# One more buffer in each ring of gathered expert rows, its room taken from the scratch of the dynamic DMAs

## What is computed

```python
def one_block(xb):                                  # xb: a block of 128 tokens
    ...
    eidx = jnp.take_along_axis(cidx, pos, axis=-1)  # 8 heads x 16 experts of 16384, per token
    gate = jax.nn.softmax(best.astype(jnp.float32), axis=-1)
    u = expert_u[eidx]
    act = jax.nn.gelu(jnp.einsum('td,thkd->thk', xb, u).astype(jnp.float32), approximate=False)
    vv = expert_v[eidx]
    return jnp.einsum('thk,thkd->td', (gate * act).astype(xb.dtype), vv)
```

## Time and profile before

| | |
|---|---|
| median of 3 runs | 2238.71 us (2237.37 to 2243.49) |
| the profiled execution: its time | 2239.32 us |
| its span, first to last instruction | 2237.5 us |
| TensorE busy | 2163.7 us, 97% |
| VectorE busy | 1173.6 us, 52% |
| HBM traffic over the span | 411 GB/s |

### The profile page before, as it was taken

One profiled execution on the slowest core, in us unless ns is written; L12 is line 12 of the kernel. 1 busy time (PEld: TensorE's weight loads), 2 busy tenths in 40 slices (PEclk: granted clock), 3 DMA queues, 4 the chain that ended last, 5 costly groups with the idle time before them and its releaser, 6 DMA issues.

```text
span 2237.5 us, 35119 instructions
## 1 busy us (share of the span) xinstructions
PE 2163.7 (97%) x14132; PEld 1989.9 (89%) x14132; DVE 1173.6 (52%) x2085; ACT 300.4 (13%) x951; POOL 370.8 (17%) x414
## 2 busy tenths in 40 slices
PE   7999998799899999999999999999999999999997
PEld 5677776586689979999999999999999999999997
DVE  3200002844466548778786457878544444444445
ACT  2000002712220011111111012322100000000002
POOL 0000100023201012222222112222111111111210
PEclk9999999999999999999999999999999999999998
DMA  7999995299969888999999999999999999999996
GB/s 286 404 400 419 403 419 190 95 370 410 384 239 400 311 312 350 404 412 421 421 419 418 420 421 409 411 398 420 421 421 422 422 422 422 422 422 422 418 422 257
DMA packets 126062, 853.68 MB, mean 382 GB/s; under 512 B 14512, under 2 KB 24880, under 8 KB 38928
## 3 DMA queue, kind: packets, MB, share of 16 engines
q1 hardware_dynamic: 57984, 424.43, 46.7%
q0 software_dynamic: 54128, 354.58, 38.8%
q10 hardware_dynamic: 13856, 73.41, 8.0%
HBM read 838.39 MB, written 81.05 MB: 411 GB/s over the span
## 4 chain that ended last, share of the span: by engine, by line
PE 36%; DMA 35%; DVE 7%; issue 2%; ACT 1%; POOL 1%; DVEq 0%; POOLq 0%; ACTq 0%
PE low L1503 30%; DMA BIG<-expert_v,VB 28%; PE big L1503 6%; DMA BIG<-expert_u,VB 4%; DVE XT L1331 3%; DMA BIG<-kaT 2%; DMA BIG<-va 1%; ACT BIG L694 1%; DVE BIG L1318 0%; POOL BIG L585 0%; DVE CST L1043 0%; DVE BIG L1329 0%; DVE BIG L1258 0%; ACT BIG L897 0%; DVE CST L1050 0%
## 5 line engine op out<-in xcount | busy, mean ns | idle before, releaser
L1503 PE MATMUL low<-HT,WR 128*128 128x176 f32 (+3 forms) x6360 | 1080.9, 332 | 3.6 <-ACT BIG L778 3.0
L1503 PEld LDWEIGHTS low<-HT,WR 128*128 128x128 f32 x6360 | 985.4, 191 | 91.0 <-ACT BIG L778 3.1
L1331 DVE SCALAR_TENSOR_TENSOR XT<-BIG,VB,XT 128x2048 f32<-128x2048 f32 x128 | 301.0, 2352 | 341.6 <-DMA BIG<-expert_v,VB 341.5
L1503 PE MATMUL low<-BIG,WR 128*128 (+3 forms) x2616 | 431.9, 320 | 10.0 <-DMA WR<-wall 10.0
L1503 PE MATMUL big<-BIG,WR 128*128 (+3 forms) x2888 | 438.5, 307 | 2.9 <-DMA WR<-expert_v 2.2
L1503 PEld LDWEIGHTS big<-BIG,WR 128*128 128x128 f32 x2888 | 419.8, 192 | 3.2 <-issue 3.2
L1503 PEld LDWEIGHTS low<-BIG,WR 128*128 128x128 f32 x2616 | 409.5, 191 | 14.1 <-issue 10.0
L1318 DVE SCALAR_TENSOR_TENSOR BIG<-BIG 128x2048 f32<-128x2048 f32 x144 | 329.4, 2291 | 171.8 <-DMA BIG<-expert_u,VB 170.2
L599 POOL DMA_INDIRECT BIG<-expert_u,VB x144 | 167.3, 1162 | 694.3 <-DVE BIG L1318 620.8
L605 POOL DMA_INDIRECT BIG<-expert_v,VB x144 | 140.5, 976 | 584.6 <-DVE XT L1331 510.0
L987 DVE TENSOR_SCALAR BIG<-low 128x320 f32 x32 | 15.7, 492 | 264.9 <-PE low L1503 264.9
(11 more groups left out here) (232 smaller groups left out, 1115.2 us busy)
## 6 DMA issues: line engine op xcount, KB each, us to landing
WR<-uT SPq DMA_DIRECT2D x128, 1024.0 KB, 10.0
WR<-wall SPq DMA_DIRECT2D x122, 1024.0 KB, 9.1
WR<-expert_v SPq DMA_DIRECT2D x66, 1024.0 KB, 9.4
WR<-expert_v ACTq DMA_DIRECT2D x62, 1024.0 KB, 9.3
BIG<-va POOLq DMA_DIRECT2D x48, 512.0 KB, 12.8
BIG<-kaT POOLq DMA_DIRECT2D x64, 384.0 KB, 13.2
bias_scratch<-BIG ACTq DMA_DIRECT2D x1, 6128.0 KB, 175.3
WR<-bias_scratch SPq DMA_DIRECT2D x4, 1024.0 KB, 5.4
```

Of the source, the lines that this page charges most:

```text
L1331: nc.vector.scalar_tensor_tensor(out=x_tok, in0=rows_of(row), scalar=weight, in1=x_tok, op0=ALU.mult, op1=ALU.add).then_inc(s_vsum, 1)
L1503: return nc.tensor.matmul(out, lhsT, rhs, start=start, stop=stop, skip_group_check=True)
```

## The change

Both rings get one more buffer. `URING` goes from 3 to 4 and `VRING` from 4 to 5 (the four of the u ring and `h_tok`). `BIG` grows by 2048 words, 8192 bytes, per partition, and `h_tok` moves behind the fourth buffer. For that the scratch goes from 16384 to 4096 bytes per partition, so everything else moves down by 12288 bytes. No engine gets another instruction or another order of instructions. What changes is the number in two waits of GpSimd, which lets a gather be issued when the row four (five) before it is done, and the buffer and semaphore that a row uses.

```diff
-URING, VRING = 3, 4
+URING, VRING = 4, 5
...
-    nc = bacc.Bacc("TRN2", target_bir_lowering=False, num_devices=1)
+    nc = bacc.Bacc("TRN2", target_bir_lowering=False, num_devices=1, dynamic_dma_scratch_size=4096)
```

## The result

The changed kernel takes 2241.47 us (median of 20 runs, 2236.75 to 2249.51), the kernel before in the same series 2238.36 us (20 runs). The medians are 3.1 us apart. The ratio of the two series, which is what is quoted from here on, is 1.0021, with a 95% interval of 1.0012 to 1.0030: 4.7 us slower (0.0021 x 2238), between 2.7 and 6.7. It is inside the band of 0.3% and clear of zero. In all that follows, the ratios leave out two executions that took far longer than the rest, 2890.96 and 6242.41 us, both of the kernel with four buffers from gather 113 on.

The account below looks back on a forecast made before the run. TensorE and the full DMA engines were both taken to be at their limit. 2239.3 + 9.0 - 2.0 - 1.5 = 2244.8, less 0.6 for the profiled execution above the median, 2244.2, stated as 2244; range 2234 to 2250.

Parts of the forecast that it names:

- the large term: Dense u chunks before the turn: the fourth u buffer keeps the gather queue full, chunks come late, TensorE loses 9.0 us.
- 4.4 us of room: Dense u chunks: chunk 4 lands at 965.3, 4.4 us before TensorE uses it.
- the prediction's rate: Dense u chunks from chunk 4 on: a chunk lands every 4.97 us, where TensorE needs 4.773.
- The early term: Rows 0 to 10: the fourth u buffer brings rows earlier and shortens TensorE's 3.0 us stall on ScalarE, -2.0 us.
- the bound of 0: Rows 0 to 10: no gain from the fourth u buffer if chunks are late there instead.
- the second rival: Dense u chunks and rows 5 to 10: slower, the lag comes without the gains, 2247.7, up to 2250; chance 0.20.
- The term of the end: TensorE's last sums: rows ending earlier give back part of the 2.65 us wait, -1.5 us.
- The two zeros: Fifth v buffer in the v chunks and smaller scratch for GpSimd's issues: each 0 us; gathers last about 23 us.
- the chunks are not starved: Dense u chunks: VectorE's hold-ups still leave the gather queue dry, TensorE keeps pace, 2233 to 2235; chance 0.22.
- The scratch: Rival: the scratch holds up GpSimd's gathers, v rows end later by tens of us; chance 0.03.
- the same page's 436 GB/s: Dense u chunks: by this rule a pair takes 4.81 us, not 4.97, and the first term would be nil.

Follow-up runs that it names:

- the two last runs: Changed kernel with four u buffers only from gather 113 on, 0.9983; changed kernel with three for gathers 42 to 112, four elsewhere, and four v buffers, 0.9993.

## Why the prediction was right, and where its terms were off

The time came out within the range, on the slow side as forecast, and for the reason given. Part of the closeness is luck: the large term has two errors of opposite sign, told next.

**The large term, +9.0, was the right mechanism and came out at 6.8.** Each part of its reasoning has a row after: the gathers had their full half (37.82 of 75.87 MB; 48 rows at 4.89 us, where 4.97 was expected), the chunks came at 4.97 us and no faster, TensorE kept its pace until the room was used up (27 chunks, and by the numbers of the prediction 4.4 us of room and 0.197 us a chunk give 22 chunks after chunk 4), and the loss stayed to the end. What was wrong is how long it lasted. The prediction had VectorE free to run up to row 112; but at row 90 it has to wait for ScalarE, whose exponentials stand behind the GELU of chunk 55, and a VectorE that is early waits all the longer, 29.8 us instead of 3.7. Row 112 came at the old time, 1330.41, and not at 1313. That this stop is what bounded the loss is shown by the run with the later weighing: lag 10.8. That run in turn shows that 9.0 was too small for what it described. The excess can be placed: in the changed kernel the first 52 chunks take 6.1 us more than before (1204.43 - 950.11, less 52 x 4.773), where the prediction's rate makes chunk 52 5.1 us late (965.3 + 48 x 4.97 against 950.6 + 52 x 4.773), and it comes in the two places in which the chain runs through transfers, where three chunks take 15.1 and 15.8 us instead of 14.9. Why they do is open.

**The early term, -2.0, can't be sized by these runs.** The 3.0 us of the earlier trace rows, which bounded it, was one draw: with three buffers this wait was 3.0, 0.7, 2.7, 1.5 and 0.7 in five executions, 1.7 in the mean; with four it is 1.2 to 1.4, always for a chunk. The rows do come earlier, as said, and the wait passes from ScalarE to the chunks, as the bound of 0 and the second rival had it. By the waits alone the term is -0.5. In one execution it was worth more, since behind the wait of 3.0 us the granted clock fell: 0.95 over the 35 us from 700 to 735, which is 3.5 us at the lower of its levels, 1.2 GHz; the same in the run with the wait of 2.7. In the other three it was 1.00. A wider measure is the stretch from TensorE's 96 matmuls behind its wait for L657 (640.13 before, 642.78 after) to chunk 0. It takes 310.5, 304.6, 310.5, 307.6 and 304.4 us with three buffers, 307.5 in the mean, and 307.3, 304.8, 307.3, 307.4, 303.8 and 305.0 with four, 305.9 in the mean. That is -1.6, but executions of one setting lie up to 6.1 us apart with three and 3.6 with four. A part of the spread is the clock: over 820 to 850 it was granted at 0.83 to 0.94 in the first five and at 0.85 to 1.00 in the other six. The ratio of the run with four buffers early says -1.6 too, with zero inside its interval. So -2.0 is neither shown nor refuted.

**The term of the end, -1.5, held.** With three buffers in the stage of the gate maps TensorE waits 1.9 to 3.8 us before its last sums, 2.7 in the mean of five; with four it waits 1.2 in all six. From the start of its last 32 matmuls of a chunk to the end of the span it is 19.7 us in the mean of the five (18.5 to 20.4) and 17.8 in the mean of the six (17.8 to 18.0), which is -1.9. That it is the fourth u buffer from row 113 on and neither the early one nor the fifth v buffer is shown by the two last runs.

**The two zeros held**, the fifth v buffer (gathers of 23.5 us, forecast 23, one issued every 5.19 us before and after) and the scratch, and neither interval allows a cost above 2 us.

The sum with the waits as measured is 6.8 - 0.5 - 1.5 = 4.8 us; with the stretches in their place it is 6.8 - 1.6 - 1.9 = 3.3. The ratio says 4.7, and its interval holds both, so it doesn't choose between them. With the terms of the waits: for the four buffers in the dense chunks alone it is 8.6 with nothing else, and 7.8 was measured; for the later weighing 10.8 - 2.0 = 8.8, and 8.5; for three buffers there, -2.0, and -4.7 was measured, with -2.2 at the interval's edge, and -1.6 for its twin with four v buffers.

**The rivals.** That the chunks are not starved (0.22) is refuted by the chain. That the lag comes without the gains (0.20) is in part what happened: the gain of the end came, that of the start isn't shown, and the lag is smaller than its 9.0. The scratch is out. The rule of the Trainium skill that DMA engines take turns between queue rows ("DMA: Bandwidth & Descriptors", section "Queues, rings and completion order") agrees with the runs: 5.28 MB each in the same 25 us, with up to four gathers against three chunks outstanding. The prediction saw this already in the earlier trace rows, "at unequal depths", but there the gathers had three buffers and the chunks three outstanding; only the runs with four buffers show it. By the same page's 436 GB/s, an estimate as the prediction worked it out, there would have been no lag; the measured 422 GB/s decided, and the lag of 6.8 us shows how much hangs on those 3%.

## What to carry to other kernels

When the DMA engines are full, a deeper ring for one stream is a bigger share for it, taken from the others; before adding a buffer, look at how near the other stream's landings are to the time in which its ring is used up (here 13.2 us of 14.3). Once its queue no longer runs dry, a further buffer buys nothing: the fifth v buffer only made each gather last longer, 23.5 us instead of 18.2. Depth can be set per stage without any other buffer: one number in the wait that issues the transfer turned this change from 4.7 us slower to 4.7 us faster (with four v buffers the same setting came out at 1.6 us faster, with zero inside the interval, so the gain is less sure than the loss). And an engine that waits for data isn't worth serving sooner if the one that sets the end pays for it.

## What I had not expected of the hardware

A wait of TensorE of 2.7 or 3.0 us near 713 went with some 3.5 us at the lower of the two granted clocks (0.95 from 700 to 735); in the nine executions with waits of 0.7 to 1.5 us at the same place it stayed at 1.00. A row of a wait in one profile is one draw: the same wait differed by up to 2.3 us between executions whose code was the same up to there.
